# The split operands of a two-layer kernel, moved off the multiples of 512 bytes

## The reference, cut to what matters

```
h = rms_norm(x, g)
proj = h @ w_in                                   # 2048 x 16512, then split into branches
merged = sigmoid(ga)*(ya @ w_up_a) + sigmoid(gb)*(yb @ w_up_b) + sigmoid(gc)*(yc @ w_up_c)
x = x + merged @ w_o
...                                               # second layer: the same pattern, then
h2 = rms_norm(x, norm2_w)
x = x + (silu(h2 @ w_ffn_gate) * (h2 @ w_ffn_up)) @ w_ffn_down   # 2048 x 5632 and back
return rms_norm(x, final_norm_w)
```

## Time and profile before

| | |
|---|---|
| median of three runs | 2960.38 us |
| the profiled execution, its own time | 2960.85 us |
| its span in the trace | 2959.1 us |
| PE busy | 2907.4 us, 98% of the span |
| PE weight loads busy (beside PE) | 2514.0 us, 85% |
| VectorE busy | 1609.6 us, 54% |
| ScalarE busy | 1336.8 us, 45% |
| GpSimd busy | 67.2 us |
| bytes moved | 518.30 MB, mean 175 GB/s |

### The profile page before, as it was taken

How to read it: one execution, slowest core, us unless ns; L and a number is a source line. 1 busy time by engine, 2 the same in 40 slices (tenths; PEclk the granted TensorE clock), 3 DMA queues, 4 the chain that set the end, 5 groups by cost and what they waited for, 6 DMA issues and landing times.

```text
span 2959.1 us, 42670 instructions
## 1 busy us (share of the span) xinstructions
PE 2907.4 (98%) x18226; PEld 2514.0 (85%) x18226; DVE 1609.6 (54%) x1851; ACT 1336.8 (45%) x1527; POOL 67.2 (2%) x173
## 2 busy tenths in 40 slices
PE   7999999999999999999999999999999999999998
PEld 7978898888988888898998889888888888888886
DVE  4555656556656556554554466554655545545444
ACT  4443543444554454444444444444444444444443
POOL 4000000001000000000000000000000000000000
PEclk9999999999999999999999999999999999999999
DMA  6343434566665655656556555666666666666664
GB/s 200 115 143 112 132 116 136 152 190 184 224 195 182 190 163 186 194 159 189 165 163 200 165 139 161 198 197 194 197 188 186 190 192 186 190 193 201 194 195 151
DMA packets 356178, 518.30 MB, mean 175 GB/s; under 512 B 18288, under 2 KB 137220, under 8 KB 355220
## 3 DMA queue, kind: packets, MB, share of 16 engines
q1 hardware_dynamic: 355220, 512.37, 58.0%
q0 software_dynamic: 768, 3.20, 0.4%
HBM read 513.39 MB, written 2.11 MB: 174 GB/s over the span
## 4 chain that ended last, share of the span: by engine, by line
PE 94%; DVE 2%; ACT 1%; issue 1%; POOL 1%; DMA 0%; SPq 0%; DVEq 0%; POOLq 0%; ACTq 0%
PE gp L1617 23%; PE gp L1619 23%; PE gp L1618 23%; PE gp L1626 6%; PE gp L1627 6%; PE gp L1628 6%; PE ps L1792 4%; PE ps L1674 1%; PE ps L1749 1%; PE ps L1780 1%; DVE w_lo L1023 1%; POOL arena L527 0%; DVE arena L1017 0%; ACT w_hi L631 0%; PE ps L1734 0%
## 5 line engine op out<-in xcount | busy, mean ns | idle before, releaser
L1023 DVE TENSOR_TENSOR w_lo<-w_raw,w_hi 128x1024 fp32r<-128x1024 f32 (+2 forms) x976 | 1169.1, 1204 | 1001.9 <-ACT w_hi L631 998.1
L631 ACT ACTIVATE w_hi<-w_raw 128x1024 fp32r<-128x1024 f32 (+2 forms) x976 | 1010.2, 1040 | 1127.8 <-PE gp L1619 897.8
L1617 PE MATMUL gp<-w_hi,h_hi 128*128 128x512 f32 x2112 | 833.0, 394 | 1.7 <-DVE w_lo L1023 1.3
L1619 PE MATMUL gp<-w_lo,h_hi 128*128 128x512 f32 x2112 | 822.6, 390 | 0.0
L1618 PE MATMUL gp<-w_hi,h_lo 128*128 128x512 f32 x2112 | 822.3, 389 | 0.0
L1626 PE MATMUL gp<-h_hi,w_hi 128*128 128x256 f32 x1696 | 496.2, 293 | 9.5 <-DVE w_lo L1023 6.6
L1627 PE MATMUL gp<-h_lo,w_hi 128*128 128x256 f32 x1696 | 481.2, 284 | 0.0
L1628 PE MATMUL gp<-h_hi,w_lo 128*128 128x256 f32 x1696 | 481.1, 284 | 0.0
L1617 PEld LDWEIGHTS gp<-w_hi,h_hi 128*128 128x128 f32 x2112 | 396.6, 188 | 84.3 <-DVE w_lo L1023 1.7
L1619 PEld LDWEIGHTS gp<-w_lo,h_hi 128*128 128x128 f32 x2112 | 396.5, 188 | 83.4
L1618 PEld LDWEIGHTS gp<-w_hi,h_lo 128*128 128x128 f32 x2112 | 396.7, 188 | 80.5 <-issue 0.5
(11 more groups left out here) (283 smaller groups left out, 1779.4 us busy)
## 6 DMA issues: line engine op xcount, KB each, us to landing
w_raw<-in_w_in SPq DMA_DIRECT2D x384, 512.0 KB, 4.2
w_raw<-in_w_ffn_gate SPq DMA_DIRECT2D x88, 512.0 KB, 4.5
w_raw<-in_w_ffn_up SPq DMA_DIRECT2D x88, 512.0 KB, 4.4
w_raw<-in_w_ffn_down SPq DMA_DIRECT2D x88, 512.0 KB, 4.1
w_raw<-in_w_in SPq DMA_DIRECT2D x136, 256.0 KB, 3.2
w_raw<-in_w_in SPq DMA_DIRECT2D x128, 192.0 KB, 2.9
w_raw<-in_w_mem_kv SPq DMA_DIRECT2D x32, 512.0 KB, 4.3
w_raw<-in_w_o SPq DMA_DIRECT2D x32, 512.0 KB, 4.3
```

The lines of the kernel that those rows point to most:

```text
L631: act.activation(w_hi[:, slot, 0:size], w_raw[:, slot, 0:size], ACT.Copy).then_inc(sem("hi_done"), 1)
L1023: dve.tensor_tensor(w_lo[:, slot, 0:size], w_raw[:, slot, 0:size], w_hi[:, slot, 0:size].bitcast(F32), ALU.subtract)\
L1617: pe.matmul(o, xh, wh, start=(k == 0), stop=False)
L1619: ins = pe.matmul(o, xh, wl, start=False, stop=(k == last_k))
```

## The change

Three operands get an address that is not a multiple of 512 bytes: `h_hi` and `h_lo` lie 128 bytes past one, `y_hi` and `y_lo` 32 bytes past, `f_hi` and `f_lo` 192 bytes past. A gap tensor of that size, itself at a multiple of 512, stands ahead of each pair. The weight ring stays at multiples. What follows a moved tensor moves with it: `mem_lo`, `mem_first` and `arena` come 32 bytes past a multiple, and `ident`, `ones` and `blk` come 192 bytes past. To make room the arena loses half a piece (165 * 128 floats instead of 83 * 256); `l_up` moves from piece 81 to piece 18, and the DMA that fills it is issued later by GpSimd, because piece 18 is still in use by an attention until then.

```diff
@@ -178,15 +178,23 @@
         ROW = 4 * P
+        PAST = {'h': 128, 'y': 32, 'f': 192}
+
+        def sb_past(name, shape, dt, where=ctx):
+            at = PAST[name[:name.index("_")]]
+            if at:
+                sb(f"gap_{name}", [P, at // 4], F32, where, ROW)
+            return sb(name, shape, dt, where, 32 if at else ROW)
...
-        h_hi = sb("h_hi", [P, KD, T], F32R, align=ROW)
-        h_lo = sb("h_lo", [P, KD, T], F32R, align=ROW)
+        h_hi = sb_past("h_hi", [P, KD, T], F32R)
+        h_lo = sb("h_lo", [P, KD, T], F32R)
@@ -208,16 +216,16 @@
-        y_hi = sb("y_hi", [P, KB, T], F32R, y_ctx, ROW)
-        y_lo = sb("y_lo", [P, KB, T], F32R, y_ctx, ROW)
-        ARENA = 83 * 256
+        y_hi = sb_past("y_hi", [P, KB, T], F32R, y_ctx)
+        y_lo = sb("y_lo", [P, KB, T], F32R, y_ctx)
+        ARENA = 165 * 128
         with ExitStack() as mem_ctx:
-            mem_lo = sb("mem_lo", [P, KD, T], F32R, mem_ctx, ROW)
-            mem_first = sb("mem_first", [P, KD // 2, T], F32R, mem_ctx, ROW)
-        arena = sb("arena", [P, ARENA], F32, y_ctx, ROW)
+            mem_lo = sb("mem_lo", [P, KD, T], F32R, mem_ctx)
+            mem_first = sb("mem_first", [P, KD // 2, T], F32R, mem_ctx)
+        arena = sb("arena", [P, ARENA], F32, y_ctx)
         y_ctx.close()
-        f_hi = sb("f_hi", [P, KF, T], F32R, align=ROW)
-        f_lo = sb("f_lo", [P, KF, T], F32R, align=ROW)
+        f_hi = sb_past("f_hi", [P, KF, T], F32R)
+        f_lo = sb("f_lo", [P, KF, T], F32R)
@@ -307,7 +315,7 @@
-        l_down, l_up, l_v = area(80, T), area(81, 512), area(56, 2, BW)
+        l_down, l_up, l_v = area(80, T), area(18, 512), area(56, 2, BW)
@@ -593,7 +601,6 @@
             pool.wait_ge(sem("cross_lo"), 12)
-            pool.dma_start(l_up[0:16, :], dram["gla_w_up_2"].rearrange("l r n -> (l r) n")).then_inc(sem("up_landed"), 16)
@@ -609,6 +616,7 @@
             pool.wait_ge(sem("y_lo"), KB + 20)
+            pool.dma_start(l_up[0:16, :], dram["gla_w_up_2"].rearrange("l r n -> (l r) n")).then_inc(sem("up_landed"), 16)
             pool.memset(l_at[:, :, :], 0.0)
```

## The result

The changed kernel took 3003.05 us (median of three runs, 3002.67 to 3006.37) against 2960.38 us before. The ratio is 1.0146, with a 95% interval of 1.0129 to 1.0163. So it is slower by 42.7 us, where I had forecast 2925 and a range that ended at 2990. In the profiled execution, the longest of the three (3006.37 us), the span grew from 2959.1 to 3004.6 us, by 45.5 us.

A forecast was written before the change was run, and what follows sets the result against it. PE, busy 98% of the span, was taken as the bound, mostly by its weight-stream matmuls. The span of 2959.1 less 35 us, other terms 0, gave 2924.1, with 1.75 us around it and rounding 2925; range 2835 to 2990.

The forecast's parts named there:

- Part (a): Relative offset of the two operands in all 14,016 stream matmuls: 2.5 ns off each, -35 us, all on the path.
- The hoped-for 10.2 ns: Part of each stream matmul's pitch, neither streaming nor a transpose's fixed cost; at best all of it goes, -143 us.
- "same time" rival: Stream pitch: 13.1 ns belong to float32r, or the readers settle alike at any offset; 2960.4 us, chance 0.20.
- The rival "slower": Lines 1617 to 1619: off zero offset, rows stay at the unsettled 231.1 ns; net +28 us, 2988, chance 0.32.
- (b): If PE gets faster, VectorE and ScalarE keep over a microsecond of slack per unit; the whole gain is kept.
- (c): Small float32 matmuls on arena, ident, ones, blk: at most 1.5 us either way, taken as 0; VectorE and ScalarE 0.
- (d): Later DMA of l_up on GpSimd: lands by 1559.2 us, reader 132 us later; cost 0, without that cover 2.4 us.
- The four readings: Pitch of line 1617 in down product, ffn stretch and up products, and of line 1626: right if falling 1 to 5 ns.

The follow-up runs named there:

- experiment three: Network left out, matmul streams alone: stationary operand at sixteen distances in 32-byte steps, behind three lead-ins; 256 columns at distance 0 gave 120.00 ns in all passes.
- experiment five: Against the changed kernel: activations back at multiples of 512, weights of 190 of 232 256-column units 64 bytes further; 2950.48 us, ratio 0.9968 to the kernel before.
- m1_offsets: Network left out: streams of 240 float32r matmuls alone at chosen operand offsets; 512 columns took 226.7 to 234.3 ns by distance, 256 columns 113.3 to 120.0 ns.

## Why the prediction was wrong

**Part (a), the step that failed.** "I take 2.5 ns off each", 14,016 x 2.5 = -35 us, where the groups gained 44 us. The term came from plain float32 rows of 275 and 272 ns. The measured changes are +5.6 ns for h, +6.4 for y, +6.8 for the memory rows, +2.2 for f and -1.0 for the 256-column form. The analogy was void. In plain float32 the distance changes nothing where it was measured (215.83 at 0, 96 and 192 bytes), and the transposes of line 1742 stayed at 272 ns when the distance between `arena` and `ident` went from 64 to 160 bytes. So the 3 ns did not come from addresses. They did not come from the column counts of the rows either (line 2000 streams 64, the transposes 128), for line 1991, no transpose, with 128 columns and both operands in the arena, has 275 too. The warning that a transpose is not quite the same operation was the thing to act on.

**The hoped-for 10.2 ns.** I had split the pitch rightly into streaming and a rest, and asked rightly whether the rest moves. But I took it for removable, where the microbenchmark has 226.67 ns as the lowest of all distances: with 512 streaming and 128 stationary columns distance 0 is the best of those measured, and any other but 256 is worse. It belongs to float32r, which the "same time" rival had named as a possibility. The Trainium skill (page "TensorE: Matmul & The Clock Gate", section "Back-to-back issue gap") gives N/2.4 + 2.5 ns for a matmul taken by itself, by which I estimate 215.8 ns for 512 columns, and about 131 ns in a stream. The bfloat16 stream here met the first figure within 0.1 ns and float32r missed it by 10.8; no run shows 131 ns.

**The rival "slower".** This was the mechanism: off distance 0 the rows form stays at about its unsettled pitch, and its place was right. Its price was 28 us against some 44. The rows form was put at +39 us and cost +44.8; the other form was put at -11 us and gave some -5 us in its steady matmuls, -0.8 by all its lengths. The first term was short because the nine matmuls of the earlier trace rows, at 231.1 ns, are below the 232.4 to 233.3 of a stream that stays off. The second took 2.1 ns from nine matmuls at distance 0, where no stream stays at 117.8 (120.0 in all three passes of experiment three). At its new distance, 384, the form has 118.7 or 120.0 alone, and 118.8 in the network. I gave this case 0.32, and put only about a tenth above 2990.

Could alone have moved the odds? Equal lengths in all records meant that distance 0 already had a settled pattern, and the only unsettled rows at hand for the form with 64% of the matmuls were slower. But equal lengths do not say that a pattern is the best one: the 256-column form had them too, and there no other distance was slower than 0.

**Parts (b) to (d).** Part (b), that a faster PE keeps its whole gain, was not tested by this change, since PE got slower. ScalarE's waits for PE rose from 897.8 to 937.2 us, so the slack is there. The test is experiment five, where 5.1 of 15.5 us were not kept, though most of that can't be told from variation. Parts (c) and (d) held. Lines 1682 and 1742 (1674 and 1734 before) stayed at 272 ns, as in the earlier trace rows. The waits, the two lines, and the later DMA with its issue, its landing time (last number) and its reader, beside the earlier trace rows:

```profile
ACT w_hi L639 <- PE gp L1627: 937.2, 582, 4.7
```

```profile
L1682 PE MATMUL ps<-ident,f_t 128*128 128x128 f32 x88 | 11.4, 272 | 0.0
L1742 PE MATMUL ps<-ident,arena 128*128 128x128 f32 x64 | 8.3, 272 | 0.0
```

```profile
1574.21 0.56 POOL L619 DMA_DIRECT2D arena<-in_gla_w_up  x1 [71.76 <-DVE y_lo L1246]
...
arena<-in_gla_w_up POOLq DMA_DIRECT2D x1, 32.0 KB, 2.0
...
L1974 PE MATMUL ps<-arena x8: 374/374/478, 1712.2 to 1713.8; 16*128 16x256 f32 x8
```

It is issued at 1574.21 us, lands 2.0 us later, and its reader comes at 1712.2, 136 us behind. The kernel without offsets, at ratio 0.9998 (0.9988 to 1.0008), puts (d) and the smaller arena at nothing within some 3.5 us. It doesn't speak for (c), since there `arena` and `ident` lie as before. For (c), all matmuls outside the stream (4,210 of them) sum to 0.6 us more length in the changed kernel than before.

**What would show it.** The four readings did their work: lengths that rise, and vary within a steady stretch, were named as the sign of "slower".

**What stays open.** That the distance within 256 bytes sets the pitch of float32r matmuls (512 streaming and 128 stationary columns) is shown, with the size for each. What inside TensorE makes it is not: of the three types tried only float32r shows it, it depends on the numbers of columns, is not the other engines, and is not one pair of reads taken alone. How to hold the 256-column form in its better state throughout was not found either.

## What to carry to other kernels

In a float32r stream with 512 streaming and 128 stationary columns put the two operands at offsets whose difference is a multiple of 256 bytes; every other difference measured cost 2 to 8 ns a matmul, and moving both by the same amount did not matter. That does not carry to other shapes: with 256 streaming columns distance 0 was the slowest (120.0 ns), with 64 stationary columns 96 bytes was better than 0, and with 384 streaming columns it made no difference. Before taking the part of a pitch that isn't streaming for waste, run the one pair of operands in a loop of its own over the offsets: one such run would have given the pitches of the rows form here within 0.3 ns. For the 256-column form it was off by 1.2 ns (120.0 against 118.8), so vary what runs before the loop as well. And when lengths in a trace are equal to the nanosecond, the pattern is settled, but whether it is the best one only other offsets can tell.

## What the runs showed that I had not expected

- The same 256-column matmuls at 64 or 320 bytes have two steady states, 113.3 and 117.8 ns, picked by what ran before, and a state once entered mostly lasts: of the shifted units straight behind a shifted one of the fast state 59 of 64 stayed in it. So a pitch from a microbenchmark need not be the one in the kernel (115.5 and 116.6 ns were the means there).
- With 384 streaming columns the distance has no effect: 173.3 ns at 0, 96 and 192 bytes. Per column, 256 columns cost 0.469 ns at distance 0, 384 cost 0.451 and 512 cost 0.443.
- A plain float32 matmul of 256 columns shows two records, each with a pitch of 215.83 ns, as long as 512 columns of bfloat16.
- On one core, with nothing but matmuls, the granted clock was 0.666 in one run and 0.995 in the next run of the same kernel, on another chip. The chip of the first had granted 0.999 to `m1_offsets`, whose span of 1721.7 us is nearly all matmuls. What made the difference no run here shows.
